# A gated DeltaNet stage: silu by one Tanh, inverse roots by Newton steps on GpSimd

## The reference

```
proj = xn @ w_in
qkv  = silu(causal_depthwise_conv(proj[..., :QKV_W], conv_w))      # 4 taps
z    = proj[..., QKV_W:QKV_W + VAL_W]
q = l2norm(q) * DK ** -0.5 ;  k = l2norm(k)      # x * rsqrt(sum(x * x) + 1e-6)
beta = sigmoid(b_logit);  g = -exp(a_log) * softplus(a_logit + dt_bias)

# per head and chunk, gcum = cumsum(g)
a_low = strict_lower(beta * (k @ k.T) * exp(gcum_i - gcum_j))
u, w  = solve(I + a_low, [v * beta, k * beta * exp(gcum)])
v_new = u - w @ S
o     = (q * exp(gcum)) @ S + (q @ k.T * gam) @ v_new
S     = S * exp(gcum_last) + (k * exp(gcum_last - gcum)).T @ v_new

o = rmsnorm(o, o_norm) * silu(z);   return o @ w_out
```

## Time and profile before

| | before |
|---|---|
| runs | 2747.92, 2749.91, 2754.03 us |
| profiled execution | 2746.65 us, span 2744.9 us |
| TensorE, busy | 2481.8 us, 90% of the span |
| VectorE | 1667.5 us, 61% |
| ScalarE | 1128.3 us, 41% |
| GpSimd | 456.6 us, 17% |
| steady stretch of the second stage (581.9 to 1511.6) | 929.7 us, TensorE 898.81 |
| opening, items 2 to 7 (220.3 to 532.6) | 312.3 us, TensorE 259.49 |

### The profile page before, as it was taken

One profiled execution on the slowest core, in us unless ns is written; L12 is line 12 of the kernel. 1 busy time (PEld: TensorE's weight loads), 2 busy tenths in 40 slices (PEclk: granted clock), 3 DMA queues, 4 the chain that ended last, 5 costly groups with the idle time before them and its releaser, 6 DMA issues. The chain is left out here.

```text
span 2744.9 us, 46422 instructions
## 1 busy us (share of the span) xinstructions
PE 2481.8 (90%) x17193; PEld 2189.3 (80%) x17193; DVE 1667.5 (61%) x3904; ACT 1128.3 (41%) x3326; POOL 456.6 (17%) x345
## 2 busy tenths in 40 slices
PE   5468888899999999999999699999996999999997
PEld 4467877789998999999999568878885777777775
DVE  4367777767777777777777322333331676666764
ACT  5244554544444444444444244433331333333332
POOL 0133333300000000000000012100001333233331
PEclk9789999999999999999999599999997999999998
DMA  6664454544446344444443167743456222222221
GB/s 199 203 248 146 140 176 149 180 138 134 141 149 203 123 149 138 126 164 134 135 158 100 34 198 264 240 159 141 171 197 254 69 71 87 83 70 82 70 71 48
DMA packets 273920, 394.24 MB, mean 144 GB/s; under 512 B 79282, under 2 KB 187906, under 8 KB 273442
## 3 DMA queue, kind: packets, MB, share of 16 engines
q1 hardware_dynamic: 240066, 370.05, 40.2%
q10 hardware_dynamic: 33632, 21.26, 2.7%
HBM read 267.92 MB, written 123.31 MB: 143 GB/s over the span
## 5 line engine op out<-in xcount | busy, mean ns | idle before, releaser
L1229 PE MATMUL p_psp<-xg,p_whi 128*128 128x264 f32 x4096 | 843.6, 295 | 27.3 <-POOL p_wlo L1178 17.2
L1229 PEld LDWEIGHTS p_psp<-xg,p_whi 128*128 128x128 f32 x4096 | 655.9, 191 | 31.8 <-issue 29.3
L1229 PE MATMUL p_psp<-xg,p_wlo 128*128 128x264 f32 x2048 | 606.6, 296 | 0.0
L1229 PEld LDWEIGHTS p_psp<-xg,p_wlo 128*128 128x128 f32 x2048 | 391.8, 191 | 0.0
L981 DVE SCALAR_TENSOR_TENSOR p_acc<-p_proj,p_taps,p_acc 128x528 f32<-128x528 f32 x288 | 243.8, 847 | 4.6
L1824 PE MATMUL first_q<-first_w,p_o 128*128 128x512 f32 (+1 forms) x864 | 205.8, 397 | 16.4 <-DVE first_w L1788 16.4
L2366 PE MATMUL first_q<-first_w,p_hT 128*128 128x512 f32 x720 | 194.8, 410 | 13.0 <-DVE p_q L2252 12.6
L1824 PEld LDWEIGHTS first_q<-first_w,p_o 128*128 128x128 f32 (+1 forms) x864 | 156.9, 184 | 58.6 <-issue 13.8
L2366 PE MATMUL p_pso<-p_wo,p_oT 128*128 128x512 f32 x768 | 193.2, 402 | 7.9 <-DVE p_oT L2278 4.2
L862 ACT ACTIVATE p_sig<-p_sig 128x528 f32<-128x528 f32 x128 | 82.6, 645 | 283.5 <-DVE p_sig L983 283.5
L1824 PE MATMUL p_psz<-p_wk,p_o 128*128 128x512 f32 x768 | 181.2, 392 | 0.0
(11 more groups left out here) (263 smaller groups left out, 4711.4 us busy)
## 6 DMA issues: line engine op xcount, KB each, us to landing
p_whi<-w_dram SPq DMA_DIRECT2D x92, 512.0 KB, 3.9
p_wlo<-w_dram SPq DMA_DIRECT2D x92, 512.0 KB, 4.8
raw<-w_a_in SPq DMA_DIRECT2D x36, 512.0 KB, 6.9
w_dram<-p_whi SPq DMA_DIRECT2D x34, 512.0 KB, 4.1
w_dram<-p_wlo SPq DMA_DIRECT2D x34, 512.0 KB, 5.4
p_o<-hT_dram SPq DMA_DIRECT2D x34, 512.0 KB, 4.9
hT_dram<-p_hT SPq DMA_DIRECT2D x32, 512.0 KB, 3.4
p_hT<-hT_dram SPq DMA_DIRECT2D x30, 512.0 KB, 4.2
```

The source lines that it names most:

```text
L1229: ins = nc.tensor.matmul(ps_p[half_][:, 0:HALF], (w_hi, w_lo)[i][:, f, kc * P:(kc + 1) * P], xg[:, g % 2, j, kc, half_ * HALF:(half_ + 1) ...
```

## The change

Silu is written with silu(x) = x/2 (1 + tanh(x/2)). ScalarE makes one Tanh with scale 0.5 from the convolved values; VectorE makes (tanh + 1) x in one operation, for all four of keys, values, queries and gate. The results are twice silu; keys and queries have their norms corrected by 0.25, 4 times the epsilon, and the gate by half the gain. The clip is left out. The Tanh stands in slots 9, 19, 22 and 1 of a step, the products in 10, 20, 23 and 3.

The inverse roots leave ScalarE. For the keys, VectorE forms the squared norm, its reciprocal, and a seed of the inverse root by integer arithmetic on the bits; GpSimd makes three Newton steps of four linked operations and one product. For the output, VectorE makes three linked operations and GpSimd three Newton steps; the scaling by ScalarE is a stage of its own, "scale", two slots after "norm". "close" and "store" stand one slot later.

```diff
-        TAPS = {7: (0, 0, (0, 1)), 8: (0, 0, (2, 3)), 9: (0, 0, (4,)), 13: (0, 1, (0,)), 14: (0, 1, (1,)),
...
-        SILU = {11: (0, 0), 21: (0, 1), 0: (1, 2), 5: (1, 3)}
+        TAPS = {7: (0, 0, (0, 1)), 8: (0, 0, (2, 3)), 13: (0, 1, (0,)), 14: (0, 1, (1,)),
+                16: (0, 1, (2,)), 18: (0, 1, (3,)), 20: (0, 2, (0, 1)), 21: (0, 2, (2, 3))}
+        TANH = {9: (0, 0), 19: (0, 1), 22: (0, 2), 1: (1, 3)}
+        SILU = {10: (0, 0), 20: (0, 1), 23: (0, 2), 3: (1, 3)}
...
                     put(0, "norm", b[0], 0)
-                    put(2, "close", b[0], 0)
-                    put(4, "store", b[0], 0)
+                    put(2, "scale", b[0], 0)
+                    put(3, "close", b[0], 0)
+                    put(5, "store", b[0], 0)
...
-                put(16, "close", main, 0)
-                put(18, "store", main, 0)
+                put(17, "close", main, 0)
+                put(19, "store", main, 0)
...
                 put(12, "norm", b[-1], 0)
+                put(14, "scale", b[-1], 0)
...
         @block.scalar
...
-            def sigmoid(it, f, part):
...
+            def half_angle_tanh(it, f):
+
+                if f < 3:
+                    act.wait_ge(conv_done, 3 * it + (f + 1))
+                else:
+                    act.wait_ge(proj_read, 2 * NF * it + 2 * NF)
+                if not (isinstance(it, int) and it == 0 and f < 2):
+                    act.wait_ge(silu_done, NF * it + (f - 1))
+                src = acc[:, f % 2, :] if f < 3 else proj[:, 1, 3:3 + GW]
+                nc.scalar.activation(sig[:, f % 2, :], src, ACT.Tanh, scale=0.5).then_inc(tanh_done, 1)
...
-                elif stage == "kk":
-                    l = lnk[:, p.which, 0:n]
-                    act.wait_ge(k_squared, k + 1)
-                    link(nc.scalar.activation(l, ssq[:, p.which, 0, 0:n], ACT.Ln, bias=cst[:]))
...
-                elif stage == "norm":
+                elif stage == "scale":
                     act.wait_ge(ms_ready, k + 1)
-                    r = o_ms[:, 0:n]
-                    link(nc.scalar.activation(r, r, ACT.Ln))
-                    link(nc.scalar.activation(r, r, ACT.Exp, scale=-0.5))
                     if not zero(k):
                         act.wait_ge(oT_ps, k)
                     for c in range(n):
                         nc.scalar.activation(o_n[:, c, :], o_of(p, c), ACT.Copy,
-                                             scale=o_ms[:, c:c + 1]).then_inc(o_read, 1)
+                                             scale=root[:, 1, 1, c:c + 1]).then_inc(o_read, 1)
...
-            nc.scalar.preload_act_table_set(LN_EXP)
+            nc.scalar.preload_act_table_set(TANH_EXP)
...
             def convolve(it, f, part):
...
-                else:
-                    nc.vector.tensor_scalar(v, src, -40.0, None, ALU.max).then_inc(conv_done, 1)
...
             def silu(q, it, f, b):
...
-                nc.vector.tensor_tensor(dst[:, P:P + TC], src[:, META:GW], sig[:, f % 2, META:GW],
-                                        ALU.mult).then_inc(silu_done, 1)
+                nc.vector.scalar_tensor_tensor(dst[:, P:P + TC], sig[:, f % 2, META:GW], 1.0, src[:, META:GW],
+                                               ALU.add, ALU.mult).then_inc(silu_done, 1)
...
                 elif stage == "low":
+                    squared = n2[:, p.which, 0:n]
                     nc.vector.tensor_copy(e_last[par][:, p.which, 0:n], mine[:, 4, 0:n])
-                    dve.wait_ge(norm_ready, 2 * k + 1)
-                    nc.vector.scalar_tensor_tensor(nD[par][:, p.which, 0:n], rn2[:, p.which, 0:n], -1.0,
+                    link(nc.vector.tensor_scalar(squared, ssq[:, p.which, 0, 0:n], 0.25, L2_EPS, ALU.mult, ALU.add))
+                    link(nc.vector.reciprocal(rn2[:, p.which, 0:n], squared))
+                    nc.vector.scalar_tensor_tensor(nD[par][:, p.which, 0:n], rn2[:, p.which, 0:n], -0.25,
                                                    mine[:, 1, 0:n], ALU.mult, ALU.mult).then_inc(scaled, 1)
...
                     last.then_inc(low_ready, 1)
+                    if not zero(k):
+                        dve.wait_ge(norm_ready, k)
+                    if not zero(p.first):
+                        dve.wait_ge(vs_ready, p.first)
+                    link(nc.vector.tensor_scalar(root[:, 0, 0, 0:n], squared, -0.5, None, ALU.mult))
+                    nc.vector.tensor_scalar(root[:, 0, 1, 0:n].bitcast(i32), squared.bitcast(i32), -0.5, float(ROOT_SEED),
+                                            ALU.mult, ALU.add).then_inc(norm_seeded, 1)
...
                 elif stage == "norm":
...
-                    nc.vector.scalar_tensor_tensor(o_ms[:, 0:n], o_ss[:, 0:n], 1.0 / P, o_bias[par][:, p.which, 0:n],
-                                                   ALU.mult, ALU.add).then_inc(ms_ready, 1)
+                    link(nc.vector.scalar_tensor_tensor(o_ms[:, 0:n], o_ss[:, 0:n], 1.0 / P, o_bias[par][:, p.which, 0:n],
+                                                        ALU.mult, ALU.add))
+                    link(nc.vector.tensor_scalar(root[:, 1, 0, 0:n], o_ms[:, 0:n], -0.5, None, ALU.mult))
+                    nc.vector.tensor_scalar(root[:, 1, 1, 0:n].bitcast(i32), o_ms[:, 0:n].bitcast(i32), -0.5, float(ROOT_SEED),
+                                            ALU.mult, ALU.add).then_inc(ms_seeded, 1)
...
-                        if f < 2 or not splitting[1]:
-                            silu(q, item, f, b)
+                        silu(q, item, f, b)
...
         @block.gpsimd
         def _(pool):
-            def silu(q, it, f, b):
...
+            def link(ins):
+                links[0] += 1
+                ins.then_inc(pool_chain, 1)
+                pool.wait_ge(pool_chain, links[0])
+
+            def inverse_root(kind, n, last=None):
+
+                minus_half, y, t = (root[:, kind, x, 0:n] for x in range(3))
+                for turn in range(ROOT_STEPS):
+                    link(nc.gpsimd.tensor_tensor(t, y, y, ALU.mult))
+                    link(nc.gpsimd.tensor_tensor(t, t, minus_half, ALU.mult))
+                    link(nc.gpsimd.tensor_scalar(t, t, 1.5, None, ALU.add))
+                    step_done = nc.gpsimd.tensor_tensor(y, y, t, ALU.mult)
...
+                elif stage == "low":
+                    pool.wait_ge(norm_seeded, k + 1)
+                    y = inverse_root(0, p.n)
+                    nc.gpsimd.tensor_tensor(norm[:, p.which, 0:p.n], n2[:, p.which, 0:p.n], y, ALU.mult).then_inc(norm_ready, 1)
+                elif stage == "norm":
+                    pool.wait_ge(ms_seeded, k + 1)
+                    inverse_root(1, p.n, last=ms_ready)
```

More of the change, by code:

```diff
@@ L628, in schedule @@
                 base[s].taps += [(it - back, f, n) for n in parts if item[back]]
-            for s, (back, f, parts) in SIGMOID.items():
-                base[s].sigmoid += [(it - back, f, n) for n in parts if item[back]]
+            for s, (back, f) in TANH.items():
+                base[s].tanh += [(it - back, f)] if item[back] else []
             for s, (back, f) in SILU.items():
@@ L885, in stage_of @@
                     last.then_inc(k_squared, 1)
-                elif stage == "kk":
-                    l = lnk[:, p.which, 0:n]
-                    act.wait_ge(k_squared, k + 1)
-                    link(nc.scalar.activation(l, ssq[:, p.which, 0, 0:n], ACT.Ln, bias=cst[:]))
-                    if not zero(k):
-                        act.wait_ge(scaled, k)
-                    if not zero(p.first):
-                        act.wait_ge(vs_ready, p.first)
-                    nc.scalar.activation(rn2[:, p.which, 0:n], l, ACT.Exp, scale=-1.0).then_inc(norm_ready, 1)
-                    nc.scalar.activation(norm[:, p.which, 0:n], l, ACT.Exp, scale=0.5).then_inc(norm_ready, 1)
                 elif stage == "tokQ":
@@ L942, in step @@
                         evacuate(item, u)
-                    for item, f, part in slot.sigmoid:
-                        sigmoid(item, f, part)
+                    for item, f in slot.tanh:
+                        half_angle_tanh(item, f)
                     for item, f, part in slot.split:
                         split_high(item, f, part)
-            nc.scalar.preload_act_table_set(LN_EXP)
+            nc.scalar.preload_act_table_set(TANH_EXP)
             act.wait_ge(const_in, 16 * N_CONST)
@@ L966, in convolve @@
             def convolve(it, f, part):
[L968 to L970 removed]
+                p, a = proj[:, f % 2, :], acc[:, f % 2, :]
+                w = taps[:, 4 * f + part:4 * f + part + 1]
+                if part == 0:
                     dve.wait_ge(proj_read, 2 * NF * it + (2 * f + 2))
@@ L1148, in _ @@
             dve.wait_ge(const_in, 16 * N_CONST)
+            link(nc.vector.tensor_scalar(gain[:], gain[:], 0.5, None, ALU.mult))
             dve.wait_ge(zeroed, 32)
@@ L1153, in _ @@
         def _(pool):
[L1154 to L1172 removed]
+            links = [0]
+            def link(ins):
```

(11 more changed lines are left out.)

86 lines of the change are left out of this document (25 added, 61 removed).

## The result

The changed kernel takes 2776.55 us in the median of four runs (2772.65 to 2778.33), the kernel before 2749.84 beside it: a ratio of 1.009, 95% interval [1.0075, 1.0105]. It is slower by 0.9%, where 2747 was forecast, and lies above the range (2725 to 2773). The profiled execution's span is 2775.9 us, 31.0 longer than before.

A forecast was written before the change was run, and what follows sets the result against it. TensorE was taken to set the pace, other engines counting only through its gaps. Steady -18, opening +13, clock +5, start -3, late inverse -2, tail +2 sum to -3: 2747 us in the median, range 2725 to 2773.

The forecast's parts named there:

- Steady items: Second stage: key and state waits gained, r and X cost, 0.82 us an item; -18 over 22 items (-27 to -4).
- -2 for items 8 and 16: Late inverse by DMA: these items start about a microsecond earlier; -2 us (-6 to 0).
- The waits for r and for X: Steady items: new TensorE waits behind the query product and the norm's extra VectorE operations, 0.2 us each.
- The link: One linked GpSimd operation of a Newton chain: 0.25 us, range 0.18 to 0.45.
- The stall in the opening: Items 2 to 7: scaling behind 25 GpSimd links delays the Xt copy; +2.3 us per item (+0.6 to +7.3).
- the 13 of the sum: Six opening items: Xt stall and the rest of the item together, 2.15 us each, +13 us.
- +0.55 a step: Opening items: query and gate products moved from GpSimd to VectorE ahead of r, less the max; +0.55 us.
- The clock in the opening: Six opening items: dry spells lower TensorE's clock, 1.6 us lost each, some already there; +5 us (0 to 10).
- The slower rival: Opening queue decides: 0.35 us a link, +4.8 in each of six items, clock 10; about 2768 us, chance 0.23.
- The tail: Last scaling: seeds and 12 links replace Ln and Exp, +2.9, late inverse gives about 1 back; +2 us (0 to +5).
- The first two items: Start of the second stage: each silu on the path two ScalarE passes shorter; -3 us (-6 to +1).

The follow-up runs named there:

- The later scaling: Changed kernel with the opening's scaling in slot 16 instead of 14, behind the first Xt copy on ScalarE; 2741.5 us, ratio 0.9965 to the kernel before.
- the three moves: Changed kernel with, in the opening, output's Newton chain first and keys' main chain behind the split; query product behind r throughout: 2736.4 us, ratio 0.9945 to before.

## Why the prediction was wrong

**Steady items: right in mechanism, and in size partly by luck.** -18 was forecast, and -2 for items 8 and 16; items 9 to 31 gave -20.3 and item 8 +0.7. Keys and state were gained as worked out. The waits for r and for X, put at 0.2 each, didn't come, so most items gained 1.0 to 1.2 instead of 0.82. Against that, the -2 didn't come: the late inverse by DMA in item 16 went from 2.1 to 4.4 us. As for r: with the Tanh undone its wait comes, at 0.4: the step that bounds r is the query product's input, and one pass makes it early enough.

**The link: nearly right.** 0.25 was taken, 0.26 to 0.34 measured, 0.29 in the mean. The wait for VectorE that I allowed for shows in single links: the one at 374.73 took 0.56 and ended at 375.29, and VectorE's tap beside it ran from 374.47 for 0.76, to 375.23:

```profile
374.47 0.76 DVE L960 SCALAR_TENSOR_TENSOR p_acc<-p_proj,p_taps,p_acc 128x528 f32<-128x528 f32 x1
```

The whole chain of 25, from 370.31 to 377.61, took 7.3 us, or 0.29 a link, and the one long link is about 0.4 us of them (0.56 instead of 0.20). In the other five opening items the longest link of this chain took 0.54 to 0.78, each beside a tap of VectorE. The other direction, of which the prediction showed one row, is in every steady item of the kernel before: the 32x64 product of VectorE took 1.07 to 1.08 beside GpSimd's query product. In the changed kernel, where that product of GpSimd isn't beside it, it takes 0.26 in the mean.

**The stall in the opening: right in place, too small in size.** +2.3 a step was forecast, 3.3 to 3.7 came; 25 links of 0.04 more make 1.0 of the difference. All of TensorE's idle time in the opening rose by 15.5 against the 13 of the sum, but that they are so near is luck. The wait for r rose by 16.6 us, where +0.55 a step, 3.3, had been allowed; and the waits for values and for ScalarE's copies, 17.3 together, went, which the sum didn't have. Of r's rise the query product is 5.9 to 8.7 us by the runs; the rest is open.

**The clock in the opening: the step that failed.** The term "+5 (0 to 10)" was mis-sized: it measured 29, and the 24 too little are most of what the forecast missed. I took one stretch behind one wait, 3.4 us at 0.52, as the price of a fall, and let only some items have one. In the changed kernel each item has two such lumps, and the one before Xt goes with 10.2 us at half clock, not 3.4: half of the 9.37 us that TensorE was busy in them, 4.7, for a wait of 3.3. The later scaling, which takes away that wait and leaves GpSimd alone, gives 24.4 us of busy time back with the same matmuls, and 10.4 of idle time.

The slower rival had the place and the sign right, with 0.23; it wanted 0.35 a link for it, an estimate of mine between the 0.18 of the earlier trace rows and the 0.46 of the earlier trace rows, and allowed 10 us for the clock. At 0.29 a link its own point, 25 links above 0.26, was already passed.

**The tail**: +2 was forecast, and from the last projection to the first matmul of the third stage +1.7 came (66.2 instead of 64.5). It isn't made up as forecast. The wait for the last scaling went from 2.4 to 5.7, as worked out (+2.9); the late inverse, of which I had expected 1 us back, waits 4.4 instead of 1.9; the rest of that stretch is 4.1 shorter.

**Outside the changed stage.** The first two items gained 3.7 where -3 was forecast. But the first stage took 4.1 us longer in this execution and the stages behind the second 3.9 longer, 8 of the 31.0 together. The change touches none of them; why they took longer is open. In the profiled executions of the other variants the second stage began at 124.9 to 128.7, and the stages behind it took 1171.6 to 1173.9 us, against 1169.0 in the kernel before.

## What to carry to other kernels

When a change moves a wait of TensorE, price the clock with it: a lump of 3.3 us before Xt cost more at half clock (4.7) than while it lasted, and the third step of eight links cost 2.2 us of waiting an item and 3.7 of clock, the fourth 2.4 and 0.8. The chain of tiny linked operations was cheap here (0.29 each) once the copy of Xt no longer stood behind its reader on ScalarE's queue: the scaling had to move two slots, and by the ratios 34 us came back. Undo such a change move by move: with the Tanh kept and three entries of the order changed, the kernel runs at 0.9945 of the one before.

## What the runs showed that I had not expected

TensorE's clock followed how its waiting lay, and not how much there was: the kernel before is idle 52.8 us in the opening and has 0.99, the three moves leave 47.4 idle and have 0.96. In the first, no wait but one is over 2.3 us; in the second, r waits up to 3.2. The length of the single wait doesn't settle it, though: a wait of 3.35 for Xt went with 10.2 us at half clock, and waits of 4.59 and 5.21 for r with 3.4 and 6.8. In the three moves the half clock doesn't even stand behind r. It begins 11.7 us before the end of the wait for r, and the waits in the 10 us ahead of it are 0.9 us and less:

```profile
364.80:368.20 3.40, 3.32 (x18) 3.20 (x19) 1.62 (x6) 0.77 (x2) 2.62 (x9) 0.50 0.94 349
```

```profile
376.45 0.35 PE L1344 MATMUL p_psc<-p_r,p_Xt 128*128 128x128 f32 x1 [2.76 <-DVE p_r L1099]
```

What decides how long the half clock lasts stays open here. The runs show its price before Xt: with two, three and four Newton steps the waits for Xt of about 1.3, 3.5 and 5.9 us went with nothing, 10.2 and 13.7 us at half clock.
